# Merged units take their tile pairs in sets of 3, 3, 2 and 2, 3, 3; four extra streams ahead of the recurrence's gates

## The reference

```python
def second_block(x, mem, ...):
    for l in range(2):
        x = x + 0.5 * swiglu_2(rmsnorm(x, ffn1_norm[l]), ffn1_w_gate[l], ffn1_w_up[l], ffn1_w_down[l])   # gua, dna
        proj = rmsnorm(x, mix_norm[l]) @ w_in[l]    # xr, yr, q, kvlru, gates (3072 columns), cq
        ...
        x = x + merged @ w_out[l]
        x = x + 0.5 * swiglu_2(rmsnorm(x, ffn2_norm[l]), ffn2_w_gate[l], ffn2_w_up[l], ffn2_w_down[l])   # gub, dnb
```

## Time and profile before

| what | value |
|---|---|
| time, median of 3 runs (lowest, highest) | 2412.74 us (2411.22, 2414.16) |
| profiled execution: time, span | 2409.69 us, 2407.9 us |
| TensorE streams (PE) busy | 2370.9 us, 98% of the span |
| TensorE weight loads (PEld) busy | 2029.7 us, 84% |
| DVE busy | 1557.6 us, 65% |
| ACT busy | 1209.4 us, 50% |
| PE in the chain that ended last | 84% |
| granted TensorE clock | 1.000 |

### The profile page before, as it was taken

One profiled execution on the slowest core, in us unless ns is written; L12 is line 12 of the kernel. 1 busy time (PEld: TensorE's weight loads), 2 busy tenths in 40 slices (PEclk: granted clock), 3 DMA queues, 4 the chain that ended last, 5 costly groups with the idle time before them and its releaser, 6 DMA issues.

```text
span 2407.9 us, 39768 instructions
## 1 busy us (share of the span) xinstructions
PE 2370.9 (98%) x14322; PEld 2029.7 (84%) x14322; DVE 1557.6 (65%) x2316; ACT 1209.4 (50%) x1783; POOL 158.1 (7%) x145
## 2 busy tenths in 40 slices
PE   8999999999999999999999999999999999999999
PEld 6756888888898868888888899998888889989887
DVE  5386665423474267766876858777677776777875
ACT  4365422222353234655554586565455556865553
POOL 3000100000000000000000013100000000221000
PEclk9999999999999999999999999999999999999999
DMA  9453755433363214656656655366566565545654
GB/s 332 135 184 128 228 154 162 143 107 96 99 193 96 88 53 154 204 163 195 201 173 193 192 168 176 130 181 193 178 191 193 180 196 167 183 130 158 200 174 149
DMA packets 388420, 398.39 MB, mean 165 GB/s; under 512 B 17344, under 2 KB 382432, under 8 KB 388304
## 3 DMA queue, kind: packets, MB, share of 16 engines
q1 hardware_dynamic: 381984, 377.67, 50.8%
q0 software_dynamic: 6320, 19.17, 2.6%
HBM read 395.73 MB, written 1.05 MB: 165 GB/s over the span
## 4 chain that ended last, share of the span: by engine, by line
PE 84%; DVE 5%; ACT 4%; issue 3%; POOL 2%; SPq 1%; DMA 1%; DVEq 0%; ACTq 0%; POOLq 0%
PE acc L1086 30%; PE acc L1097 23%; PE acc L1090 16%; PE acc L1163 2%; PE wk L1163 2%; ACT w_hi L1689 1%; DVE w_lo L2328 1%; SPq L795 1%; PE wk L1285 1%; PE acc L1639 1%; PE wk L1323 1%; PE acc L1323 1%; PE wk L1305 1%; POOL bias L994 1%; PE wk L1534 1%
## 5 line engine op out<-in xcount | busy, mean ns | idle before, releaser
L2328 DVE TENSOR_TENSOR w_lo<-raw,w_hi 128x1024 fp32r<-128x1024 f32 (+1 forms) x656 | 815.9, 1258 | 496.9 <-ACT w_hi L1689 495.1
L1689 ACT CAST w_hi<-raw 128x1024 fp32r<-128x1024 f32 (+1 forms) x650 | 663.8, 1034 | 466.8 <-PE acc L1097 346.1
L1086 PE MATMUL acc<-h_room,w_hi 128*128 128x512 f32 x2328 | 584.6, 393 | 2.0 <-DVE h_room L2579 0.8
L1097 PE MATMUL acc<-h_room,w_lo 128*128 128x256 f32 (+1 forms) x3688 | 562.0, 294 | 0.0
L1097 PEld LDWEIGHTS acc<-h_room,w_lo 128*128 128x128 f32 x3688 | 515.5, 188 | 44.7
L1086 PEld LDWEIGHTS acc<-h_room,w_hi 128*128 128x128 f32 x2328 | 415.5, 188 | 79.0 <-DVE h_room L2456 3.3
L1090 PE MATMUL acc<-h_room,w_hi 128*128 128x256 f32 (+1 forms) x2720 | 464.6, 323 | 3.2 <-POOL h_room L999 2.2
L1090 PEld LDWEIGHTS acc<-h_room,w_hi 128*128 128x128 f32 x2720 | 399.9, 188 | 47.7 <-issue 6.6
L1086 PE MATMUL acc<-hid_all,w_hi 128*128 128x512 f32 x880 | 221.4, 392 | 0.0
L1086 PEld LDWEIGHTS acc<-hid_all,w_hi 128*128 128x128 f32 x880 | 156.7, 188 | 26.7
L1097 PEld LDWEIGHTS acc<-hid_all,w_lo 128*128 128x128 f32 x1056 | 152.3, 188 | 16.7
(11 more groups left out here) (439 smaller groups left out, 2300.6 us busy)
## 6 DMA issues: line engine op xcount, KB each, us to landing
raw<-in_w_in_dram SPq DMA_DIRECT2D x100, 512.0 KB, 4.0
raw<-in_ffn_w_in_dram SPq DMA_DIRECT2D x88, 512.0 KB, 4.4
raw<-in_ffn_w_gate_dram SPq DMA_DIRECT2D x88, 512.0 KB, 4.2
raw<-in_ffn_w_up_dram SPq DMA_DIRECT2D x88, 512.0 KB, 4.3
raw<-in_ffn_w_down_dram SPq DMA_DIRECT2D x80, 512.0 KB, 4.0
raw<-in_ret_w_qkvg_dram SPq DMA_DIRECT2D x48, 512.0 KB, 3.6
raw<-in_ffn_w_out_dram SPq DMA_DIRECT2D x40, 512.0 KB, 3.5
ring<-in_ada_w_dram SPq DMA_DIRECT2D x34, 512.0 KB, 4.7
```

The source lines that it names most:

```text
L1086: pe.matmul(outs[cb], w_hi[:, s, k, c], merged[:, :, kk, t], start=(u == 0 and k == 0), stop=False, skip_group_check=True)
L1097: mm = pe.matmul(o, w_lo[:, s, k, cb * P:(cb + 1) * P], x[:, u * KCH + k, t], start=False, stop=(last and k == nk - 1), skip_group_check=True)
L1689: act.copy(w_hi[:, s, 0:nk, :], raw[:, s, 0:nk, :]).then_inc(hi_done, 1)
L2328: dve.tensor_tensor(w_lo[:, s, 0:nk, :], raw[:, s, 0:nk, :], w_hi[:, s, 0:nk, :], ALU.subtract).then_inc(lo_done, 1)
```

## The change

A merged unit that doesn't open is no longer eight streams of 512 and then eight of 256. It is cut into sets: so many streams of 512, then as many of 256 for the same tiles, then the next set. `set_sizes` gives the sizes: 3, 3, 2 and 2, 3, 3 by turns; 4, 2, 2 for the first unit behind the opening ones, and for the first unit of each iteration of a loop that has no iteration written out ahead of it (and then 2, 3, 3 goes on); 2, 2 for a unit of half size. The wait for `lo_done` moves to behind the first set's streams of 512. In iterations of the loop after the first one, the two units that opened now take sets as well. Ahead of the first stream of `gates` stand two streams of 256 and two of 512 columns whose result is overwritten.

```diff
+            def set_sizes(job, first, p, anew):
+                good, sizes = True, []
+                for q in range(first, p + 1):
+                    if job.unit_chunks[q] < KCH:
+                        sizes = [2, 2]
+                    elif q == first and anew:
+                        sizes, good = [4, 2, 2], False
+                    else:
+                        sizes, good = [3, 3, 2] if good else [2, 3, 3], not good
+                return sizes
...
+                        if primed and isinstance(it, int) and p == 0:
+                            for x in (slice(0, 1), slice(0, 1), slice(0, 2), slice(0, 2)):
+                                pe.matmul(acc[:, 0, 0, 0:(x.stop - x.start) * S], w_hi[:, s, 0, 0:P], h_all[:, x, 0, tok], start=True, stop=True,
+                                          skip_group_check=True)
...
-                            opens = b == 0 and ((normed is not None and not isinstance(normed, tuple)) or (scaled is not None and isinstance(it, int)))
+                            opened = isinstance(it, int) and ((normed is not None and not isinstance(normed, tuple)) or scaled is not None)
+                            opens = b == 0 and opened
+                            if merged is not None and not opens:
+                                pairs = [(k, cb) for cb in range(2) for k in range(nk)]
+                                sizes = set_sizes(job, per if opened else 0, p, isinstance(it, int) or not (sums or busy or free))
+                                for g, n in enumerate(sizes):
+                                    some = pairs[sum(sizes[:g]):sum(sizes[:g]) + n]
+                                    for k, cb in some:
+                                        pe.matmul(outs[cb], w_hi[:, s, k, cb * P:(cb + 1) * P], merged[:, :, u * KCH + k, t],
+                                                  start=(u == 0 and k == 0), stop=False, skip_group_check=True)
+                                    if not g:
+                                        unit_ready(job, l, it, p)
+                                    for k, cb in some:
+                                        mm = pe.matmul(outs[cb][:, S:2 * S], w_lo[:, s, k, cb * P:(cb + 1) * P], merged[:, 0, u * KCH + k, t],
+                                                       start=False, stop=(last and k == nk - 1), skip_group_check=True)
+                                mm.then_inc(units_used, 1)
...
-                elif sums or busy:
+                elif sums or busy or (primed and job.iters > 1):
...
-                product("gates", l, free=[job.taken(l, 0, 2), job.taken(l, 0, 3)])
+                product("gates", l, primed=True, free=[job.taken(l, 0, 2), job.taken(l, 0, 3)])
```

More of the change, by code:

```diff
@@ L1024, in keep_busy @@
                     pe.matmul(bank[:, 0:P], ident[:, :], ident[:, :], start=True, stop=True, skip_group_check=True)
+            def set_sizes(job, first, p, anew):
[8 more added lines that the diff above has]
+                return sizes
             def product(name, l=None, hi=None, lo=None, tok=slice(0, S), rows_of=None, needs=None, normed=None, squared=False,
                         after=None, scaled=None, sums=None, merged=None, free=None,
-                        sums_after=None, written=False, by_columns=False, busy=0):
+                        sums_after=None, written=False, by_columns=False, busy=0, primed=False):
                 job = J[name]
@@ L1076, in one @@
                             outs = [acc[:, b % 2, cb, 0:t.stop - t.start] if merged is None else acc[:, b % 2, cb, :] for cb in range(2)]
-                            opens = b == 0 and ((normed is not None and not isinstance(normed, tuple)) or (scaled is not None and isinstance(it, int)))
+                            opened = isinstance(it, int) and ((normed is not None and not isinstance(normed, tuple)) or scaled is not None)
[14 more added lines that the diff above has]
+                                mm.then_inc(units_used, 1)
+                                if after:
+                                    after(it * job.body + p)
+                                if sums and isinstance(it, int) and p == 1:
+                                    pooled_sum(*sums)
+                                continue
                             order = [(k, cb) for k in range(nk) for cb in range(2)] if opens else [(k, cb) for cb in range(2) for k in range(nk)]
```

## The result

The changed kernel took 2417.59 us (median of 11 runs, 2415.58 to 2419.41), the kernel before 2411.41 us in the same job (12 runs, 2410.64 to 2414.16): a ratio of 1.0023, with a 95% interval of 1.0015 to 1.0031. It is slower by about 0.2%; the 0.2% that the prediction took as the least difference from no change that it can tell lies inside the interval. The forecast was 2417.3 us. It was made on a base of 2412.74; against the 2411.41 of this job the forecast step of +4.6 us stands beside a measured one of +6.2, so 1.3 us of the close hit is owed to the base. (A twelfth run of the change, 7821 us, and one of the experiments, 3368 us, were disturbed and are left out.)

The account below looks back on a forecast made before the run. The prediction took TensorE's distances between stream starts as the bound. Sets +3.2, first part 0 and streams ahead of gates +1.4 gave +4.6 us on 2412.74, so 2417.3 us, range 2404.5 to 2419.5.

Parts of the forecast that it names:

- The mechanism: On TensorE, stream order decides whether 256-column streams run in step or out of step, 4.2 us per thousand streams apart.
- The first part: rg, rwo, gu1 and dn1, entered behind norm stalls: between -1.1 and +1.2 us, taken as 0.
- The rule of places: Fitted rule for TensorE: streams of 512 and 256 move a place between 0 and 3; only place 0 is in step.
- entered wrongly: In gua and gub, 2, 3, 3 begins at place 0: 14 of 16 256s out of step, 25 ns more a pair.
- the 1.58 us a layer: Cost of sets in a later layer: 1.28 us for 51 pairs, 0.15 each for dna and dnb; 3.2 for two layers.
- the earlier wait: Waiting for lo_done up to 1.4 us earlier in merged units costs nothing while DVE is a unit ahead.
- rival A: All products in step, gates too, with gains in rq and q: 10 us less, 2402.6 us; chance 0.16.
- rival E: Wrong entry in the first part's products too, +1.2 us: 2418.5 us, decided by gu1 (0.5 us); chance 0.15.
- The four streams: Ahead of gates: 0.69 us a layer, +1.4 us for two, with gates staying out of step.
- D: Pace does not depend on stream order, only added streams count: +1.4 us, 2414.1 us; chance 0.12.
- B: Sets entered wrongly, gates in step: -0.6 us, 2412.1 us; chance 0.12.
- C: Sets entered rightly, gates out of step: -4.9 us, 2407.8 us; chance 0.20, half of it mixed entries.

Follow-up runs that it names:

- the mended entry: The changed kernel without the streams ahead of gates, first sets of gua, gub, dna, dnb and memk turned over: 2409.31 us, ratio 0.9989 to the kernel before.
- the second profile of the change: The changed kernel, unaltered, run and profiled once more: 2415.04 us, one run.
- the kernel with the three edits: The changed kernel with later layers' sets entered rightly, dn1's units whole and three streams (256, 512, 512) ahead of gates: 2404.97 us, ratio 0.9970 to the kernel before.

## Why the prediction was right

The mechanism held, and so did the entries on which the sum rests. The first part's zero and 1.3 us of the nearness to the measured time are luck. The rule of places stays a fit: it carried the order through all the sets and through three and four streams ahead of gates, and was not clear for a single 512.

**The sets.** gua and gub were entered wrongly, in every profile of the change, and dna, dnb and memk inherited it. From gua's sums to the next ones, behind gua, dna and memk, the kernel before takes 188.98 us in both layers, the change 189.67 in both (its second one from 1777.0 to 1966.7), the mended entry 187.90 in both. By the prediction's own prices gua's 21 pairs, memk's 2 and dna come to 0.73 us there; measured were 0.69. gub with dnb, without the small products around them, came to 0.68 by those prices and measured 0.7 (183.9 to 184.6 us from sums to sums). xr and yr, priced at 0.18, were entered behind a stall of xr's norm and did not always come out alike: yr took 22.05 us before, 22.19 in one layer of either profile of the change and 22.04 in the other. So the 1.58 us a layer held to about 0.2. All sets together cost 3.8 us by the run with them alone, for 3.2 forecast.

**The term that was mis-sized** is the earlier wait, costed at 0. The prediction named its cover, a unit that DVE is ahead, and took it from an idle time of 0.0, which belongs to a kernel in which nobody asked early. At one unit of dn1 a 2.29 us operation of the norm had eaten that cover, and the set asked 1.4 us earlier than the unit had. It cost 0.44 us by itself, and 0.2 to 0.7 with the place that it left TensorE at.

**The first part** was taken as 0 between -1.1 and +1.2. By the second profile of the change it is 0.0 (1137.81 against 1137.78 us), made of terms that cancel. From the sums ahead of rg to those ahead of gu1 it takes 1.1 us less, of which 0.85 are rq in step, as rival A priced it; gu1 takes 0.4 us more, since it is entered wrongly, which was rival E's condition (priced at 0.5); dn1 takes 0.7 us more, the wait in it. The forecast had put rq's gain with the right entries only. rq was in step in five of the six profiles of kernels with sets and in one of the four without, so the sets may favour it, but no run shows that they cause it.

**The four streams** cost 0.71 us a layer, for 0.69 forecast, and did not catch gates, which by the rule is entered at place 2. With three streams it is caught, and the 2.6 us less a layer that the prediction gave for that were 2.68 - 0.12 = 2.56.

**What was left over.** The two parts by themselves add up to 3.8 + 0.9 = 4.7 us, the forecast's 4.6, and lie within the interval of the change's own ratio (3.6 to 7.5 us). The runs that timed the change itself gave 6.2; the single later run gave 2415.04, 3.4 us over the kernel before beside it. Nothing in the traces speaks for a further step of 1.5 us. Entries that differ from profile to profile (rq 0.85 us, dn1 0.5, q 0.42, yr 0.15) could make scatter of this size; that they do stays open.

**The rivals.** D, that the order is worth nothing, falls with the mended entry: the same streams, 6.4 us apart. The Trainium skill, "TensorE: Matmul & The Clock Gate", section "Back-to-back issue gap", gives N/2.4 + 2.5 ns as the distance of an isolated matmul of N columns when warm. That makes 109 ns for 256 columns, an estimate from its formula; here streams of 256 columns that follow each other at a granted clock of 1.00 ran at 113.3 or 117.8 ns, and no run has an isolated one. A had everything in step, gates too; the kernel with the three edits comes nearest to it, 6.7 us under the kernel before, where A had 10, with gu1 still wrong, dn1 as before, and gates caught but lost again near its end. B and C each had either gates or the sets entered rightly, and the change has neither. Of E, gu1's wrong entry came true, and the sum of the first part did not.

## What to carry to other kernels

Where TensorE is the bound and never waits, read the distances from start to start of equal streams: if they come in two values, the order of unlike streams is worth time, and so is the place at which a product is entered. A pattern of period two that keeps itself up keeps a wrong entry up too; derive the entry of each product from the trace and set it by the product, as the kernel with the three edits does in the later layers, or leave the order alone. Behind a stall of varying length even that isn't sure: rq took 21.76 or 22.61 us and yr 22.04 or 22.19, from profile to profile. An idle time of 0.0 says that nobody asked too early so far, not how much earlier one may ask: look for the longest operation that ever stands ahead of the one waited for.

## What the runs showed of the hardware

At one granted clock, 1.00, streams of 256 columns that follow each other ran 113.3 or 117.8 ns apart, and kept their pace through a whole product of 576 streams, over the ends of units and of loops, until a wait of 0.41 us changed it. Three streams ahead of the product, 256, 512 and 512 columns, moved it from the slower to the faster. Sets of 3, 3, 2 and 2, 3, 3 kept all but two of each sixteen 256s at the faster pace or all but two at the slower, by the order of their first sets alone: 120.71 or 121.89 us for 44 units. What in the engine has this memory, no run shows. One split on DVE took 5.65 us while it overlapped an operation of GpSimd of 5.53 us, where most take 1.22, and every split of over 1.5 us in that trace overlaps one of GpSimd; not every overlapping split is long, and what decides it was not tested.
